# Mixture-of-experts output: expert rows scaled on leaving PSUM and added to the residual in HBM by indirect DMA

## The reference

```
h = rms_norm(x, norm_g)                                # (1024, 1024)
grp = argmax(g_logits); g_w = softmax(g_logits)[grp]   # 4 groups
top_val, top_local = top_k(e_logits, 2)                # 2 of 8 experts in the group
e_w = softmax(top_val) * g_w                           # weight of each of the two
# rows of one expert are put together in blocks of 128
y_rows = (silu(xb @ w_gate[e]) * (xb @ w_up[e])) @ w_down[e]
y = segment_sum(y_rows * row_w[:, None], row_tok)      # each token sums its two rows
x = x + y
```

## Time and profile before

| | us |
|---|---|
| median of three timed runs | 1659.43 |
| the three runs | 1656.99, 1659.43, 1665.18 |
| span of the profiled execution, first to last instruction | 1660.4 |

### The profile page before, as it was taken

How to read it: one execution, slowest core, us unless ns; L and a number is a source line. 1 busy time by engine, 2 the same in 40 slices (tenths; PEclk the granted TensorE clock), 3 DMA queues, 4 the chain that set the end, 5 groups by cost and what they waited for, 6 DMA issues and landing times. The chain is left out here.

```text
span 1660.4 us, 17595 instructions
## 1 busy us (share of the span) xinstructions
PE 1436.3 (87%) x6162; PEld 885.5 (53%) x6182; DVE 573.4 (35%) x1140; ACT 402.3 (24%) x990; POOL 193.0 (12%) x242
## 2 busy tenths in 40 slices
PE   4899999999967768999999599999729999999980
PEld 2445544554534667788887255566514444444440
DVE  0234223323345326655554113334551111111115
ACT  1121112111112534554443013233201111111110
POOL 0012012201210002111100000000011110110104
PEclk8899999999988658999999699999859999999995
DMA  9110001001207620100040310210155999999948
GB/s 366 47 38 26 19 32 38 25 13 38 64 31 260 230 70 26 52 27 27 24 193 8 118 51 4 73 39 26 39 177 189 366 372 364 372 371 365 370 151 304
DMA packets 125755, 224.16 MB, mean 135 GB/s; under 512 B 6016, under 2 KB 82048, under 8 KB 125568
## 3 DMA queue, kind: packets, MB, share of 16 engines
q1 hardware_dynamic: 118640, 197.69, 33.9%
q0 software_dynamic: 7056, 25.69, 4.1%
HBM read 181.42 MB, written 41.94 MB: 135 GB/s over the span
## 5 line engine op out<-in xcount | busy, mean ns | idle before, releaser
L432 PE MATMUL pj<-arena,xT 128*128 128x512 f32 (+1 forms) x768 | 318.5, 572 | 2.2 <-DMA arena<-in_w_in 2.0
L432 PEld LDWEIGHTS pj<-arena,xT 128*128 128x128 f32 x768 | 146.3, 194 | 155.4 <-issue 150.2
L1709 PE MATMUL egu<-arena,exT 128*128 128x512 f32 x512 | 227.6, 598 | 1.2 <-issue 1.2
L1709 PEld LDWEIGHTS egu<-arena,exT 128*128 128x128 f32 x512 | 95.7, 192 | 110.4 <-issue 109.8
L1108 DVE TENSOR_REDUCE anm<-asc 128x1 f32<-128x640 f32 (+7 forms) x128 | 90.5, 707 | 121.9 <-PE asc L1012 121.2
L1069 ACT ACTIVATE ap<-asc,anm 128x640 f32<-128x640 f32 (+7 forms) x128 | 89.7, 701 | 157.9 <-DVE anm L1108 147.4
L1697 PE MATMUL eyp<-arena,ehT 128*128 128x512 f32 x256 | 115.2, 593 | 1.0 <-ACT ehT L1740 1.0
L1267 PE MATMUL xpj<-arena,xTA 128*128 128x512 f32 x256 | 113.9, 604 | 0.7 <-ACT xTA L1334 0.7
L233 ACT ACTIVATE raw<-pj 128x512 f32<-128x512 f32 (+1 forms) x48 | 27.1, 564 | 271.9 <-PE pj L432 271.9
L1767 DVE TENSOR_TENSOR eh<-esg,egu 128x256 f32<-128x256 f32 x32 | 13.5, 421 | 220.2 <-ACT esg L1746 220.2
L1023 PE MATMUL atp<-early,ap 128*128 128x128 f32 x528 | 82.9, 281 | 5.1 <-ACT apT L1080 4.4
(11 more groups left out here) (321 smaller groups left out, 1978.2 us busy)
## 6 DMA issues: line engine op xcount, KB each, us to landing
arena<-in_w_gate SPq DMA_DIRECT2D x32, 1024.0 KB, 7.5
arena<-in_w_up SPq DMA_DIRECT2D x32, 1024.0 KB, 9.8
arena<-in_w_down SPq DMA_DIRECT2D x32, 1024.0 KB, 11.6
y_d<-ey SPq DMA_DIRECT2D x32, 512.0 KB, 9.9
arena<-in_w_in SPq DMA_DIRECT2D x6, 2048.0 KB, 18.6
x<-in_x SPq DMA_DIRECT2D x16, 512.0 KB, 4.2
y_d<-arena SPq DMA_DIRECT2D x2, 4096.0 KB, 18.7
rope<-in_rope SPq DMA_DIRECT2D x8, 512.0 KB, 3.5
```

The lines of the kernel that those rows point to most:

```text
L432: last = nc.tensor.matmul(dst[:, 0:n], xT[:, k, :], w[c][:, k, :], start=k == 0, stop=k == KT - 1)
L1709: last = nc.tensor.matmul(gu[k % 2][:], xT[k % 2][:, c, :], m.gateup[k][:, c, :], start=c == 0, stop=c == KT - 1)
```

## The change

- In `phase_mix` SP also stores each finished tile of the residual to a new HBM tensor `acc_d` (1024 rows and 128 spare ones), ahead of the store of `h_d`. The filling of `y_d` during attention is gone.
- `phase_route` now works out the weights of the two experts of a token, splits them in three bfloat16 parts, and lets POOL and PE bring them into the order of the item rows (`m.wrow`). Places without a token get weight 0, the gather index 0, and in the new table `m.to` a spare row of `acc_d` of their own.
- In `phase_experts`, `keep_y` multiplies by the column of `m.wrow` while it copies. SP's store to `y_d` is replaced by `add` on POOL: an indirect DMA with `compute_op=ALU.add` that adds the 128 rows of `ey` to rows `m.to` of `acc_d`. Each add waits for the one before to have landed, since two items can hold rows of the same token.
- `phase_combine` is gone. After the last add, SP copies 4 MB from `acc_d` to the output in one DMA.

```diff
-                    if i == NT - 1:
-                        sp.wait_ge(m.w_out_in, 48)
-                        spare = m.y_d.rearrange("(b k p) d -> b p k d", p=P, k=KT)
-                        for b in range(NE // KT, MAXI // KT):
-                            sp.dma_start(spare[b], m.w_out).then_inc(s["spare"], 16)
                 store(NT - 2)
-                sp.wait_ge(s["spare"], 32)
...
                     if 0 <= t < NT:
+                        sp.wait_ge(s["x2"], 2 * t + 2)
+                        sp.dma_start(av[t], m.x1[:, t, :]).then_inc(s["kept"], 16)
                         sp.wait_ge(s["h3"], t + 1)
                         sp.dma_start(hv[t], h3[:]).then_inc(s["h3out"], 16)
...
+            @block.gpsimd
+            def _(pool):
+                pool.wait_ge(s["hits"], 1)
+                for j in range(3):
+                    pool.wait_ge(s["parts"], j + 1)
+                    nc.gpsimd.tensor_tensor(whot[:, :, j], hits[:], bc(flat(part[j]).unsqueeze(2), [P, 2 * NT, MAXI]),
+                                            ALU.mult).then_inc(s["whot"], 1)
...
                 last.then_inc(s["mapped"], 1)
+                pe.wait_ge(s["whot"], 3)
+                for n in range(2 * NT):
+                    last = nc.tensor.matmul(wm[:, 0:3 * MAXI], rhot[:, n, :], whot[:, n].rearrange("p a i -> p (a i)"),
+                                            start=n == 0, stop=n == 2 * NT - 1)
+                last.then_inc(s["weighed"], 1)
...
+                dve.wait_ge(s["exps"], 1)
+                done(red(gw[:], gs[:], AX.X, ALU.add))
+                done(nc.vector.reciprocal(gw[:], gw[:]))
+                done(ts(rec[:], d[:], 1.0, None, ALU.add))
+                done(nc.vector.reciprocal(rec[:], rec[:]))
+                done(tt(wts[:, 0, :], gw[:], rec[:], ALU.mult))
+                done(tt(wts[:, 1, :], wts[:, 0, :], d[:], ALU.mult))
+                nc.vector.tensor_copy(part[0][:], wts[:]).then_inc(s["parts"], 1)
+                dve.wait_ge(s["parts"], 1)
+                done(tt(left[:], wts[:], part[0][:], ALU.subtract))
+                nc.vector.tensor_copy(part[1][:], left[:]).then_inc(s["parts"], 1)
+                dve.wait_ge(s["parts"], 2)
+                done(tt(left[:], left[:], part[1][:], ALU.subtract))
+                nc.vector.tensor_copy(part[2][:], left[:]).then_inc(s["parts"], 1)
...
-                done(tt(hits[:], bc(m.c("item").unsqueeze(1), [P, 2 * NT, MAXI]),
-                        bc(flat(item).unsqueeze(2), [P, 2 * NT, MAXI]), ALU.is_equal))
+                tt(hits[:], bc(m.c("item").unsqueeze(1), [P, 2 * NT, MAXI]),
+                   bc(flat(item).unsqueeze(2), [P, 2 * NT, MAXI]), ALU.is_equal).then_inc(s["hits"], 1)
+                dve.wait_ge(s["hits"], 1)
...
-                done(nc.vector.scalar_tensor_tensor(m.slot[:], item[:], float(P), row[:], ALU.mult, ALU.add))
                 dve.wait_ge(s["mapped"], 1)
-                done(nc.vector.tensor_copy(hits[:, 0, :], rm[:, 0:MAXI]))
-                done(nc.vector.scalar_tensor_tensor(m.rows[:, 0:MAXI], rm[:, MAXI:2 * MAXI], float(P), hits[:, 0, :],
+                tok = maps[:, 0, :]
+                done(nc.vector.tensor_copy(maps[:, 1, :], rm[:, 0:MAXI]))
+                done(nc.vector.scalar_tensor_tensor(tok, rm[:, MAXI:2 * MAXI], float(P), maps[:, 1, :],
                                                     ALU.mult, ALU.add))
-def phase_experts(nc, m, io):
+                done(ts(maps[:, 1, :], tok, -1.0, None, ALU.add))
+                done(ts(m.rows[:, 0:MAXI], maps[:, 1, :], 0.0, None, ALU.max))
+                done(nc.vector.scalar_tensor_tensor(maps[:, 2, :], tok, 0.0, bc(m.c("unused"), [P, MAXI]), ALU.is_equal,
+                                                    ALU.mult))
+                done(tt(m.to[:, 0:MAXI], maps[:, 1, :], maps[:, 2, :], ALU.add))
+                dve.wait_ge(s["weighed"], 1)
+                done(nc.vector.tensor_copy(maps[:], wm[:, 0:3 * MAXI].rearrange("p (a i) -> p a i", a=3)))
+                done(tt(maps[:, 0, :], maps[:, 0, :], maps[:, 1, :], ALU.add))
+                done(tt(m.wrow[:], maps[:, 0, :], maps[:, 2, :], ALU.add))
...
             @block.sync
             def _(sp):
                 last_round = rounds(sp)
-                def store(b, k):
-                    sp.wait_ge(s["y0"], 4 * b + k + 1)
-                    sp.wait_ge(s["y1"], 4 * b + k + 1)
-                    sp.dma_start(yv[4 * b + k], y[k % 2][:]).then_inc(kept[k % 2], 16)
+                sp.dma_start(m.acc_d[S:S + P], io["x"][0:P]).then_inc(s["cleared"], 16)
                 with sp.Fori(0, last_round) as b:
                     for k in range(SLOTS):
                         e = sp.value_load(m.experts[0:1, bass.ds(4 * b + 4 + k, 1)], min_val=0, max_val=NE - 1)
                         sp.wait_ge(s["down"], 4 * b + k + 1)
                         load_expert(sp, m, io, e, k)
-                        store(b, k)
-                for k in range(SLOTS):
-                    store(last_round, k)
+                sp.wait_ge(s["added"], 64 * last_round + 64)
+                sp.dma_start(out.rearrange("b s d -> (b s) d"), m.acc_d[0:S]).then_inc(s["out"], 16)
+                sp.wait_ge(s["out"], 16)
...
+                def add(b, k):
+                    nc.gpsimd.tensor_copy(to[k][:], m.to[:, bass.ds(4 * b + k, 1)]).then_inc(s["to"], 1)
+                    pool.wait_ge(s["y0"], 4 * b + k + 1)
+                    pool.wait_ge(s["y1"], 4 * b + k + 1)
+                    if not (isinstance(b, int) and b == 0 and k == 0):
+                        pool.wait_ge(s["added"], 64 * b + 16 * k)
+                    pool.wait_ge(s["to"], 4 * b + k + 1)
+                    nc.gpsimd.tensor_tensor(mark[:], to[k][:], to[k][:], ALU.add).then_inc(s["mark"], 1)
+                    nc.gpsimd.indirect_dma_start(m.acc_d, bass.IndirectOffsetOnAxis(to[k][:], 0), y[k % 2][:], None,
+                                                 compute_op=ALU.add).then_inc(s["added"], 16)
                 for k in range(SLOTS):
                     gather(0, k, k < 2)
-                with pool.Fori(1, last_round + 1) as b:
+                pool.wait_ge(s["cleared"], 16)
+                for k in range(SLOTS):
+                    gather(1, k)
+                    add(0, k)
+                with pool.Fori(2, last_round + 1) as b:
                     for k in range(SLOTS):
                         gather(b, k)
+                        add(b - 1, k)
                 gather(last_round + 1, 0)
+                for k in range(SLOTS):
+                    add(last_round, k)
                 pool.wait_ge(got[0], 32 * last_round + 48)
-                for p in range(2):
-                    pool.wait_ge(kept[p], 32 * last_round + 32)
...
-            def keep_y(eng, half, copy, b, k, sem_):
+            def keep_y(eng, half, scaled, b, k, sem_):
                 eng.wait_ge(s["down"], 4 * b + k + 1)
                 if not (isinstance(b, int) and b == 0 and k < 2):
-                    eng.wait_ge(kept[k % 2], 32 * b + 16 * (k // 2))
-                copy(y[k % 2][:, 512 * half:512 * half + 512], yp[half][:]).then_inc(sem_, 1)
+                    eng.wait_ge(s["added"], 64 * b + 16 * k - 16)
+                scaled(y[k % 2][:, 512 * half:512 * half + 512], yp[half][:], m.wrow[:, bass.ds(4 * b + k, 1)]
+                       ).then_inc(sem_, 1)
...
+                scaled = lambda o, a, w: nc.scalar.activation(o, a, ACT.Copy, scale=w)
...
+                scaled = lambda o, a, w: nc.vector.tensor_scalar(o, a, w, None, ALU.mult)
...
-def phase_combine(nc, m, io, out):
...
-            @block.sync
-            def _(sp):
-                ov = out.rearrange("b (t p) d -> (b t) p d", p=P)
-                for t in range(NT):
-                    sp.wait_ge(added, 2 * t + 2)
-                    sp.dma_start(ov[t], m.x1[:, t, :]).then_inc(gone, 16)
-                sp.wait_ge(gone, 16 * NT)
...
-        m.y_d = dram("y_d", [MAXI * P, D])
+        m.acc_d = dram("acc_d", [S + P, D])
```

More of the change, by code:

```diff
@@ L75 @@
 LATE, NLATE = pack([("before", 128), ("ones", 128), ("iota", 128), ("thr", 16), ("eid", 32), ("pref8", 8),
-                    ("place", 1), ("tile", 16), ("item", 48), ("thr4", 4)])
+                    ("place", 1), ("tile", 16), ("item", 48), ("thr4", 4), ("unused", 1)])
 class Chain:
@@ L941, in phase_attend @@
         s = {n: sem("a_" + n) for n in (
-            "scored nmax expd turned evac0 evac1 valued read ms rs out oout chain q_in qsplit spare").split()}
+            "scored nmax expd turned evac0 evac1 valued read ms rs out oout chain q_in qsplit").split()}
         oc_in = [sem("a_oc0"), sem("a_oc1")]
@@ L1206, in phase_mix @@
             "w_in turned evac mmA mmB mmC mmD mmE mmF x1 x2 sqA sqE msA msE msB rsA rsE rsB h1 h3 h3out qraw qn nmax "
-            "expd om lg chain late_in").split()}
+            "expd om lg chain late_in kept").split()}
         o_in = [sem("x_o0"), sem("x_o1")]
@@ L1211, in phase_mix @@
```

(37 more changed lines are left out.)

39 lines of the change are left out of this document (2 added, 37 removed).

## The result

The changed kernel takes 1663.86 us (median of 11 runs), the one before 1656.88 (11 runs): the ratio is 1.0046, with a 95% interval of 1.0030 to 1.0062. That is 0.46% slower. The forecast was 1659 us against a median of 1659.43, so no change. The time lies inside the range given, 1638 to 1695, but no change was forecast and the medians differ by 7.0 us, clear of the noise.

A forecast was written before the change was run, and what follows sets the result against it. In the expert stage PE and DMA were both full, PE setting the pace by a hair. 1660.4 - 24.0 + 4.5 + 1.0 + 17.8 = 1659.7, 1.0 lower on the median's scale: 1659 us, no change, range 1638 to 1695.

The forecast's parts named there:

- The price of an add: Expert stage: DMA time of an add beyond the plain write it replaces, forecast at 1.23 us more.
- The double: Expert stage: an add takes two passes in, one out, 2.46 us against a plain write's 1.23.
- The rule cited in the prediction: Trainium skill, Collectives: the DMA adder works "read-read-write with the add free in between", so the second read costs, the double price.
- The loss in the stage: Expert stage: 34.4 us more DMA work from 28 adds, less gaps 7.0 and lead 9.6: 17.8 us lost.
- The slack of a period: Expert stage: DMA's gaps in each 11.40 us period, taken as 0.25 us, 7.0 over 28 loads.
- The lead: Expert stage: last down weights land 9.6 us before the product needing their slot starts; set against the added DMA work.
- The tail: After the last kept result: last adds and a 14 us copy replace the 45.6 us combine; 24.0 us saved (16 to 26).
- the 207 to 214 that the prediction cites: Final copy: skill's GB/s per direction between HBM tensors; by it the copy is 19.6 us, the saving about 16.
- Costed at nothing: No cost or gain from residual stores in phase_mix, attention's dropped 8 MB, scaling in keep_y, or add waits on POOL.
- the route term: Route stage: weights on DVE, three products on POOL, 16 on PE, three small DVE operations; 4.5 us lost.
- the upper bound of 8.2: Route stage: upper limit of the loss, if DVE's big operations hold POOL off, 4.3 us more.
- the clearing: Start of expert stage: SP's 0.5 MB to the spare rows beside the first gather; 1.0 us lost (0 to 1.2).

The follow-up runs named there:

- run 1: The changed kernel with plain indirect writes of the expert rows in place of the adds, queue and waits kept: 1638.60 us, ratio 0.9873.
- run 2: The kernel before, with POOL gathering each item's 128 rows once more into a tile nobody reads, no add: 1671.62 us, ratio 1.0075.
- run 6: The changed kernel with gathers that leave out the places no token takes, by an index above the bound: 1656.77 us, ratio 0.9988.
- run 3: The changed kernel with the 8 MB written during attention put back, to a buffer nobody reads: 1662.85 us, ratio 1.0040.
- run 5: The changed kernel with weights, products (on DVE) and m.to made at the expert stage's start, spare rows cleared in the output projection: 1655.09 us, ratio 0.9981.
- run 12: The changed kernel with POOL's route products after all four parts of rhot, and the spare rows cleared in the output projection: 1660.33 us, ratio 1.0013.

## Why the prediction was wrong, point by point

*The price of an add: right.* The double was taken, 1.23 us more; it is 1.4 (the queue rows, and run 1, where a plain write cost what a gather does). The rule cited in the prediction, that an add is two reads and a write, fits this price; no row shows the second read itself.

*The loss in the stage: right in sum, by luck.* 17.8 was forecast, 17.0 measured, and three errors cancel. The add was taken 0.2 us too cheap, which over 28 loads is 5 us too little. The slack of a period was taken 0.4 too small: 0.25, where runs 1 and 2 show 0.65 to 0.7; that is 11 us too much. The lead was taken 9.6 us and bought about 4, 6 us too little. I had called a share of 1.03 full and counted only dips below it. Bound by DMA, the changed kernel shows 1.07 and run 2 1.06; (1.07 - 1.03) / 1.07 of 11.4 us is 0.43 us, about the missing part. It is no fixed number, though: run 6 reads 1.03, and PE still waits. What the lead bought is seen from the sum: at 0.77 a period 28 loads would cost 21.6 us, and from the second gate product to the last the changed kernel took 17.4 us longer. The first down weights that the loop loads are issued at 1275.17, land 13.5 us later, and are there 7.3 us before their product starts at 1295.97. The sixth, issued at 1335.77, land 17.3 us later, just as theirs starts at 1353.19. With the queue full the loads are issued later and land later, and the lead is gone after five items.

*The tail: nearly right.* 22.1 saved for 24.0. The copy took 14.5 for 14, the last add 6.0 for 5.6; 0.9 more went to the wait for the add before, which was issued 0.9 us after its result and landed 6.3 later, for 0.5 and 5.6. The copy ran at 290 GB/s, not at the 207 to 214 that the prediction cites; the Trainium skill, DMA: Bandwidth & Descriptors, section Latency and other measured facts, gives these for rows of 16 KB that lie 512 KB or more apart, and the measurement decides.

*Costed at nothing: right as far as it shows.* Without the fill in attention nothing is won (run 3, with it, is 1.0 us faster, within the noise), and the stage of run 1 is 373.9 us with the scaled copies. No run takes the stores of the residual away; their stage took 292.4 us before (922.7 to 1215.1) and 290.7 in the changed kernel (922.0 to 1212.7).

*The step that failed is the route term:* "I take 4.5 us lost". It is 7.4. The prediction led the path from `hits` over POOL's products and PE's to the last operations of DVE, and let DVE's own operations keep their lengths beside POOL. In the trace the path is DVE's alone. POOL is done at 1233.55, 1.75 us before DVE ends `rrh`, and PE's product is done at 1237.67, 1.8 us before DVE takes it up:

```profile
1235.65 2.02 PE L1540 MATMUL rwm<-rwh,rrh 128*128 128x144 bf16 x16
...
1239.44 0.31 DVE L1637 COPY rmaps<-rwm 128x144 f32<-128x144 f32 x1
```

DVE loses 1.8 us to the weights (1.9 forecast), 3.8 to POOL beside it, and 1.7 to the added operations behind `rrh` (4.97 us for 3.25). The middle one was put at nothing: POOL held off by DVE was in the text, as the upper bound of 8.2, but not DVE held off by POOL. That 7.4 comes near that bound is chance. The term is 2.9 of the 4.8 us between the sum forecast and the terms measured; the clearing is 0.8, the tail 1.9, and the stage gives 0.8 back. Runs 5 and 12 confirm the two terms ahead of the stage: without POOL's products route is 21.4 us, and with them moved behind `rrh` DVE's operations have their old lengths.

*The rest.* The terms sum to +4.1 us, the medians differ by 7.0, and 2.9 are not placed. The profiled execution of the kernel before took longer than its median: the changed kernel's time is 1.9 us above its span (1663.86, 1662.0), and by the same difference that span of 1660.4 is a time of 1662.3, 5 above the median. It also reaches the route stage 2.4 us later than the changed kernel, among fourteen profiles that spread over 11 us at that point with nearly the same program ahead of it. So the 2.9 may be such variation of one execution. That is argued and not shown. Nor is it known why run 6 used only a third of what it freed.

## What to carry to other kernels

An accumulating DMA costs its queue a pass more than a plain write. It is free only where DMA has that much room. A share near 1 doesn't tell the room well (1.07, 1.06 and 1.03 were read here while PE waited for DMA); adding a transfer of known price and watching the period, as run 2 does, does. Where DMA and PE are both near full, make the packets of the big loads longer first: that gave the changed kernel 20.6 us and the kernel before 4, and the change, 7 us slower by itself, is worth 19.3 with it and with the edits of run 5. A few small operations on POOL beside DVE's big ones cost DVE more than doing them on DVE, and work that isn't needed for the first step of the next stage belongs in the shadow of its first transfer.

## What the runs showed that was not expected

- DVE's operations beside POOL's took 2.22 for 0.95 us and 5.03 for 2.49, and POOL's 6.26 for 4.77.
- SP's issue of weight loads in rows of 1 KB held up the barrier into the next stage: DVE waited 3.78 us there, and 0.53 with rows of 8 KB.
- POOL needs 1.57 us to issue an add of 128 rows, and 0.98 for a plain write of the same rows (run 1, `acc_d<-ey,eto`).
- One copy of 4 MB from HBM to HBM took 14.5 us, 290 GB/s, in 64 packets of 64 KB.
- A gather that skips half of its rows took half the DMA time, yet the weight loads beside it ran no faster: 350 GB/s of their own time without the skip, 346 with it (13.04 MB in 74.6% of 50 us, 13.10 in 75.8%).
